# Hybrid layers and recurrence of a 4-layer network: slab splits ahead of the latents, angles in the second network, a new order behind the last recurrent tile

## What is computed

```python
def recurrent_mixer(x, ...):
    gate, xr = jnp.split(x @ w_in, [LRU_WIDTH], axis=-1)
    xr = causal_depthwise_conv(xr, conv_w, conv_b)
    r, i = sigmoid(block_diag(gate_a_w, gate_a_b)), sigmoid(block_diag(gate_x_w, gate_x_b))
    log_a = -LRU_C * r * softplus(-a_param)
    u = sqrt(-expm1(2.0 * log_a)) * (i * xr)
    h = scan(h -> exp(log_a) * h + u)
    return (h * gelu(gate)) @ w_out

def hybrid_layer(x, positions, ...):
    h = rms_norm_2(x, g_mix)
    (a_q, a_k, a_v, b_qlat, b_kvlat, b_krope, c_q, c_k, c_v, c_f, d_val, d_gate) = split(h @ w_in)
    out_a = chunk_band_attention(a_q, a_k, a_v, rel_bias)
    q  = rms_norm_2(b_qlat, g_q_lat) @ w_uq        # 64 + 32 columns a head; the 32 are rotated
    kv = rms_norm_2(b_kvlat, g_kv_lat) @ w_ukv     # keys (b_key) and values (b_values)
    k_rot = apply_rope(b_krope, positions)         # cos and sin of positions * inv_freq
    out_b = block_causal_attention(q, [kv keys, k_rot], kv values, CHUNK)
    out_c = block_causal_attention(c_q, c_k, c_v, 1, cumsum(log_sigmoid(c_f + b_forget)))
    out_d = silu(layer_norm(depthwise_conv(d_val * sigmoid(d_gate))))
    x = x + sum(sigmoid(h @ w_gate + b_gate) * (branches @ w_branch)) @ w_o
    return x + square(relu(rms_norm_2(x, g_ffn) @ w_up)) @ w_down
```

## Time and profile before

| | us |
|---|---|
| median of 3 runs | 2874.03 (2872.92 to 2875.7) |
| the profiled execution | 2871.91 |
| its span in the profile | 2870.1 |

### The profile page before, as it was taken

One profiled execution on the slowest core, in us unless ns is written; L12 is line 12 of the kernel. 1 busy time (PEld: TensorE's weight loads), 2 busy tenths in 40 slices (PEclk: granted clock), 3 DMA queues, 4 the chain that ended last, 5 costly groups with the idle time before them and its releaser, 6 DMA issues.

```text
span 2870.1 us, 32424 instructions
## 1 busy us (share of the span) xinstructions
PE 2799.6 (98%) x12948; PEld 2267.7 (79%) x12948; DVE 1248.2 (43%) x2084; ACT 1231.1 (43%) x1803; POOL 1234.4 (43%) x550
## 2 busy tenths in 40 slices
PE   8999999999989999998999999999989999999998
PEld 7786888888768888876777888888767777888886
DVE  4666551544675335335656432021256574330112
ACT  3665442434844334324673443133235754442331
POOL 4222444444554444433445444444424564444442
PEclk9999999999999999999999999999999999999999
DMA  4211232333223333322222323333322222333332
GB/s 149 89 63 63 89 103 94 96 103 96 81 81 96 103 95 96 103 81 74 74 67 88 96 96 96 98 98 98 96 73 81 61 88 88 96 96 101 97 96 73
DMA packets 73926, 259.21 MB, mean 90 GB/s; under 512 B 9184, under 2 KB 9184, under 8 KB 73776
## 3 DMA queue, kind: packets, MB, share of 16 engines
q1 hardware_dynamic: 71680, 251.79, 27.9%
q10 hardware_dynamic: 2096, 5.36, 0.5%
HBM read 254.95 MB, written 2.13 MB: 90 GB/s over the span
## 4 chain that ended last, share of the span: by engine, by line
PE 91%; DVE 4%; ACT 3%; POOL 1%; issue 1%; DMA 0%; SPq 0%; DVEq 0%; ACTq 0%; POOLq 0%
PE ps L423 27%; PE ps L425 26%; PE ps L424 26%; PE ps L489 2%; PE ps L519 1%; PE ps L502 1%; PE ps L544 1%; PE ps L546 1%; PE ps L545 1%; PE ps L434 1%; ACT w_hi L876 1%; PE ps L471 1%; PE ps L473 1%; PE ps L472 1%; POOL w_lo L1885 1%
## 5 line engine op out<-in xcount | busy, mean ns | idle before, releaser
L1885 POOL TENSOR_TENSOR w_lo<-raw,w_hi 128x1024 fp32r<-128x1024 f32 x470 | 1133.9, 2415 | 1516.8 <-ACT w_hi L876 1516.7
L423 PE MATMUL ps<-xs,w_hi 128*128 128x512 f32 x2176 | 864.7, 397 | 14.0 <-POOL w_lo L1885 11.2
L424 PE MATMUL ps<-xs,w_hi 128*128 128x512 f32 x2176 | 849.6, 390 | 0.0
L425 PE MATMUL ps<-xs,w_lo 128*128 128x512 f32 x2176 | 849.4, 390 | 0.0
L876 ACT ACTIVATE w_hi<-raw 128x1024 fp32r<-128x1024 f32 x470 | 493.8, 1052 | 620.7 <-PE ps L425 575.6
L423 PE MATMUL ps<-hid,w_hi 128*128 128x512 f32 x1320 | 517.8, 392 | 13.6 <-POOL hid L1909 9.7
L425 PE MATMUL ps<-hid,w_lo 128*128 128x512 f32 x1320 | 515.1, 390 | 0.0
L424 PE MATMUL ps<-hid,w_hi 128*128 128x512 f32 x1320 | 514.9, 390 | 0.0
L423 PEld LDWEIGHTS ps<-xs,w_hi 128*128 128x128 f32 x2176 | 410.2, 189 | 116.7 <-issue 12.8
L424 PEld LDWEIGHTS ps<-xs,w_hi 128*128 128x128 f32 x2176 | 410.2, 189 | 88.9 <-issue 5.0
L425 PEld LDWEIGHTS ps<-xs,w_lo 128*128 128x128 f32 x2176 | 410.0, 188 | 86.2
(11 more groups left out here) (213 smaller groups left out, 2610.8 us busy)
## 6 DMA issues: line engine op xcount, KB each, us to landing
raw<-in_weights SPq DMA_DIRECT2D x470, 512.0 KB, 3.5
hT<-in_x ACTq DMA_DIRECT2D x4, 512.0 KB, 9.5
btab<-in_rel SPq DMA_DIRECT2D x8, 256.0 KB, 3.6
out<-tmp ACTq DMA_DIRECT2D x8, 256.0 KB, 2.0
btab<-in_heads SPq DMA_DIRECT2D x6, 256.0 KB, 3.7
tmp<-in_heads SPq DMA_DIRECT2D x6, 256.0 KB, 4.2
common<-in_fixed ACTq DMA_DIRECT2D x1, 642.0 KB, 12.9
small<-in_small ACTq DMA_DIRECT2D x1, 368.5 KB, 4.7
```

What stands on the lines that cost most here:

```text
L423: pe.matmul(banks[bank][:], wh, rh, start=(k == 0), stop=False)
L424: pe.matmul(banks[bank][:], wh, rl, start=False, stop=False)
L425: last = pe.matmul(banks[bank][:], wl, rh, start=False, stop=(k == len(specs) - 1))
L1885: gp.tensor_tensor(w_lo[:, n % NPAIR, :], raw[:, n % NRAW, :], w_hi[:, n % NPAIR, :].bitcast(F32), ALU.subtract).then_inc(*w_low.tick(n))
```

## The change

In the hybrid layers ScalarE gets steps `("ahead", n)`: it opens the slab of c_head n between the latents' steps; the other engines skip them. b_values moves from attention step 1 to step 2, behind c_head 4. The by-token product uses bank 4 instead of 7, and b_key 0 uses bank 4 instead of the next of the ring.

The angles and their sine move into `network(1, 3)`, between the up tiles and the down tiles of its first half, and use `pbuf` instead of `tmp`.

In the recurrence Gelu of gate 7 moves on ScalarE behind the high part of tile 7's input; tiles 6 and 7 take Exp and Sqrt together; VectorE takes `rec_1(6)` before tile 7's low part; TensorE adds inputs 3, 4 and 5 one at a time over six outputs; ScalarE and GpSimd get one order written out for all of this. TensorE's products are the same in number. Unchanged lines are left out.

```diff
-                   ("latent_parts", 1), ("latent_parts", 0), ("c_head", 1), ("c_head", 2), ("c_head", 3)]
-        beside2 = {0: [("rope", 0)], 1: [("b_key", 0), ("b_key", 1), ("b_values", 0)], 2: [("c_head", 4)],
+                   ("ahead", 1), ("latent_parts", 1), ("ahead", 2), ("latent_parts", 0), ("ahead", 3), ("c_head", 1),
+                   ("c_head", 2), ("c_head", 3)]
+        beside2 = {0: [("rope", 0)], 1: [("b_key", 0), ("b_key", 1)], 2: [("c_head", 4), ("b_values", 0)],
...
-        rec_first = {8: [(0, 0, 3), (1, 0, 3)]}
-        rec_early = {8: [(o, 0, 3) for o in range(2, 6)], 9: [(o, 3, 5) for o in range(6)],
-                     10: [(o, 5, 6) for o in range(6)]}
@@ TensorE: root_by_token @@
-                wait_bank(7)
+                wait_bank(4)
...
-                free[7] = (vec, ("by_token", m))
+                free[4] = (vec, ("by_token", m))
@@ TensorE: recurrence @@
-            for c in range(13):
-                if c < 8:
-                    rec_0(c)
-                for o, k0, k1 in rec_first.get(c, ()):
-                    rec_out(o, k0, k1)
-                if 0 <= c - 1 < 8:
+            for c in range(8):
+                rec_0(c)
+                if c:
                     rec_1(c - 1)
-                for o, k0, k1 in rec_early.get(c, ()):
-                    rec_out(o, k0, k1)
+
+            for o in range(2):
+                rec_out(o, 0, 3)
+            rec_1(7)
+            for o in range(2, 6):
+                rec_out(o, 0, 3)
+            for k in range(3, 6):
+                for o in range(6):
+                    rec_out(o, k, k + 1)
@@ TensorE: hybrid, b_key @@
-                        bk = next_bank(("b_key", L, a))
+                        if a:
+                            bk = next_bank(("b_key", L, a))
+                        else:
+                            bk = bank_of["b_key", L, a] = 4
@@ ScalarE: network @@
+                    if L == 1 and part == 0:
+                        A.wait_ge(vec, "angles")
+                        ac.activation(rp[64:128, :], pbuf[64:128, 0, :], ACT.Sin).then_inc(*act.tick("rope"))
                     for o in range(8):
                         weights(("down", L, part, o))
@@ ScalarE: recurrence (rec_t is the third Tanh, taken out of rec_1) @@
+            roots_of = {3: (0, 1), 5: (2, 3), 7: (4, 5)}
+            for c in range(8):
+                weights(("rec_g", c))
...
+                weights(("rec_x", c))
+                if c < 7:
                     rec_gate(c)
...
+                rec_in(c)
+                if c:
                     rec_1(c - 1)
+                if 0 < c < 7:
+                    rec_t(c - 1)
+                rec_high(c)
+            rec_t(6)
+            rec_gate(7)
+            rec_4(3)
+            for o in range(2):
+                weights(("rec_out", o))
+            weights(("rec_a", 7))
+            weights(("rec_i", 7))
+            rec_1(7)
+            rec_t(7)
+            rec_2((6, 7))
+            for o in range(2, 6):
+                weights(("rec_out", o))
+            for k in range(3, 6):
+                rec_4(k + 1)
+                for o in range(6):
+                    weights(("rec_out", o), k)
+            rec_4(7)
@@ ScalarE: hybrid @@
-                    elif what == "c_head":
+                    elif what in ("c_head", "ahead"):
                         weights(("c_head", L, a))
@@ VectorE: network @@
+                    if L == 1 and part == 0:
+                        angles()
                     residuals((0, 1, 2, 3) * 2, ("down", L, part), m + 1 if part else None)
@@ VectorE: rec_0, and its loop @@
                     V.wait_ge(product, ("rec_i", c - 2))
+                if c == 7:
+                    rec_1(6)
                 take_low(hi_lo(hid, 8 + c % 2), xc, ("rec_x", c))
...
+            rec_3(4)
+            rec_1(7)
+            for c in range(5, 8):
+                rec_3(c)
@@ GpSimd: recurrence, behind tile 7 @@
+            rec_4(3)
+            for o in range(2):
+                weights(("rec_out", o))
+            weights(("rec_a", 7))
+            weights(("rec_i", 7))
+            rec_3(4)
+            for o in range(2, 6):
+                weights(("rec_out", o))
+            for k in range(3, 6):
+                rec_4(k + 1)
+                rec_3(k + 2)
+                for o in range(6):
+                    weights(("rec_out", o), k)
+            rec_4(7)
```

More of the change, by code:

```diff
@@ L448, in root_by_token @@
                 T.wait_ge(inverse, ("root", m))
-                wait_bank(7)
+                wait_bank(4)
                 for b in range(NB):
-                    t = pe.matmul(banks[7][:, b:b + 1], rt[0:1, P * b:P * b + P], ones[0:1, 3, 0:1], start=True, stop=True)
+                    t = pe.matmul(banks[4][:, b:b + 1], rt[0:1, P * b:P * b + P], ones[0:1, 3, 0:1], start=True, stop=True)
                 t.then_inc(*mean.tick(("by_token", m)))
-                free[7] = (vec, ("by_token", m))
+                free[4] = (vec, ("by_token", m))
             def values(group, specs, rhs, m, bank0):
@@ L1103, in rec_1 @@
             def rec_1(c):
-                e, t, gi = ring(c)
+                e = ring(c)[0]
                 A.wait_ge(product, ("rec_a", c))
@@ L1111, in rec_1, with rec_t @@
                     *act.tick(("rec_i", c)))
+            def rec_t(c):
+                e, t, gi = ring(c)
                 A.wait_ge(vec, "softplus")
@@ L1129, in rec_4 @@
                 take_high(hid[:, c, :], tmp[:, 4 + c % 4, :], ("rec_y", c))
-            roots_of = {3: (0, 1), 5: (2, 3), 7: (4, 5), 8: (6,), 9: (7,)}
-            for c in range(13):
-                if c < 8:
-                    weights(("rec_g", c))
+            roots_of = {3: (0, 1), 5: (2, 3), 7: (4, 5)}
+            for c in range(8):
+                weights(("rec_g", c))
                 if c == 0:
@@ L1161, in scalar @@
             network(1, 3)
-            A.wait_ge(vec, "angles")
-            ac.activation(rp[64:128, :], tmp[64:128, 4, :], ACT.Sin).then_inc(*act.tick("rope"))
             def hybrid(L):
@@ L1370, in by_token @@
                     V.wait_ge(moved, event)
-                ve.tensor_copy(rtok, banks[7][:, 0:NB]).then_inc(*vec.tick(("by_token", m)))
+                ve.tensor_copy(rtok, banks[4][:, 0:NB]).then_inc(*vec.tick(("by_token", m)))
             def values_out(group, event, bank0, dst):
@@ L1569, in softplus, with angles @@
                 ve.tensor_scalar(hb[:, 8:16], small[:, gx0:gx0 + 8], 0.5, None, ALU.mult).then_inc(*vec.tick("softplus"))
+            def angles():
+                r64 = slice(64, 128)
+                ang, kk = pbuf[r64, 0, :], pbuf[r64, 1, :]
+                V.wait_ge(l_pos, "pos")
+                V.wait_ge(l_common, "common")
+                chain(ve.tensor_copy(kk, rp[r64, :].bitcast(I32)))
+                V.wait_ge(step)
+                chain(ve.tensor_scalar(ang, kk, ropec[r64, 0:1], None, ALU.mult))
+                V.wait_ge(step)
+                chain(ve.tensor_scalar(kk, ang, 1.0 / (2 * math.pi), ropec[r64, 1:2], ALU.mult, ALU.add))
+                V.wait_ge(step)
+                chain(ve.tensor_scalar(kk, kk, 12582912.0, None, ALU.add))
+                V.wait_ge(step)
+                chain(ve.tensor_scalar(kk, kk, -12582912.0, None, ALU.add))
+                c1 = 6.28125
+                c2 = float(np.float32(2 * math.pi - c1))
+                c2 = float(np.frombuffer((np.frombuffer(np.float32(c2).tobytes(), np.uint32) & 0xFFFFF000).tobytes(), np.float32)[0])
+                c3 = 2 * math.pi - c1 - c2
+                for cc in (c1, c2, c3):
+                    V.wait_ge(step)
+                    chain(ve.scalar_tensor_tensor(out=ang, in0=kk, scalar=-cc, in1=ang, op0=ALU.mult, op1=ALU.add))
+                V.wait_ge(step)
+                chain(ve.tensor_scalar(ang, ang, ropec[r64, 2:3], 3.1415925, ALU.add, ALU.min))
+                V.wait_ge(step)
+                ve.tensor_scalar(ang, ang, -3.1415925, None, ALU.max).then_inc(*vec.tick("angles"))
             def network(L, m):
@@ L1640, in rec_3 @@
                 ve.tensor_tensor_scan(att[:, 8 + c, :], t, gi, 0.0, ALU.mult, ALU.add).then_inc(*vec.tick(("rec_scan", c)))
[L1642 removed]
+            for c in range(8):
                 if c == 0:
                     root(2)
[L1645 removed]
+                if c >= 4:
                     rec_3(c - 4)
[L1647 to L1650 removed]
+                scale(2 * (c % 2), ("rec_g", c), 2, ("rec_g", c))
+                rec_0(c)
+                if 0 < c < 7:
                     rec_1(c - 1)
+            rec_3(4)
+            rec_1(7)
+            for c in range(5, 8):
+                rec_3(c)
             residuals(range(8), ("rec_out",), 3, ("rec",))
             network(1, 3)
[L1656 to L1679 removed]
             def hybrid(L):
@@ L1912, in gpsimd @@
             through(("rec_g", 0))
-            for c in range(13):
-                if c < 8:
-                    weights(("rec_g", c))
```

(17 more changed lines are left out.)

45 lines of the change are left out of this document (2 added, 43 removed).

## The result

The changed kernel takes **2852.2 us** (median of four executions, 2851.8 to 2853.4) beside 2874.1 for the kernel before. The ratio is 0.9925, with a 95% interval of 0.9913 to 0.9938. That is 22.0 us faster, where 24.4 were forecast.

The account below looks back on a forecast made before the run. TensorE, busy 98% of the span, bounds the kernel, so only its waits and low-clock stretches yield time. Gains 20.3 + 2.1 - 2.0 + 4.0 = 24.4 us off the 2874.0 median give 2849.6 us, range 2841 to 2861.

Parts of the forecast that it names:

- 1 and 2, latents and banks: Hybrid layers: slab splits ahead of the latents gain 20.3 us (17 to 23), bank moves 2.1 (1 to 2.3).
- the loss today in the first hybrid layer: End of c_head 2 to first transpose: 21 us of work in a 36.2 us window, so 15.2 us lost.
- The charge of 1.5 us of lower clock for each new wait: Behind the new wait of about 2.15 us before score 2, each hybrid layer: 1.5 us lost (0 to 3.0).
- 3, angles: Second network: old place gives back 4.1 us, new place costs 4.1 of wait plus 2.0 clock; net -2.0 us.
- 4, recurrence: End of the recurrence: tile 7's low part 5.2 us earlier, less 1.2 for lower clock; gain 4 us (0 to 6).
- Part (a): Recurrence, before tile 7's input: VectorE's low part ends 1.8 us earlier, and the wait shrinks to about 1.2 us.
- The charge of 1.2 us for the clock: Recurrence: 1.2 us taken off the gain for lower clock behind a TensorE stand of 4.4 us.
- A: Rival: splits hide the wait, nothing new appears, score 2's wait and angles cost no clock; gain about 29, 2845; chance 0.17.
- B: Rival: wait before score 2 keeps clock low, 3 us more per layer, angles 1 more; gain 17, 2857; chance 0.15.
- C: Rival: VectorE and GpSimd's shared-port lock delays the recurrence, tile 7 at 813.5; gain there 1, 2853; chance 0.10.
- D: Rival: slower, a long stretch at 1.2 GHz follows the new stand at 978; 200 slow matmuls give 2892; chance 0.03.
- E: Rival: opening slabs ahead waits for a late release, delaying the latents' high parts; gain 6, 2868; chance 0.05.

Follow-up runs that it names:

- sin_later: Changed kernel with ScalarE's Sin of the angles moved behind its second call for down-tile slabs; 2847.1 us, 25.9 faster than the kernel before.
- hybrid_alone: Kernel before with only the hybrid-layer edits (slabs opened ahead of latents, b_values later, bank 4 uses); 2853.0 us, 20.0 faster than the kernel before.
- recurrence_alone: Kernel before with only the new order of the recurrence; 2868.3 us, 4.7 faster than the kernel before.
- tile4_first: Changed kernel with tile 4's high part ahead of two slab splits and its low part ahead of both w_lo; 2851.4 us, 22.0 faster than the kernel before.

## Why the prediction was right, step by step

The forecast of 2849.6 us lies 2.6 below the measured 2852.2, and 24.4 us were forecast for a gain of 22.0.

- **1 and 2, latents and banks: forecast 22.4, alone 20.0.** Every mechanism was as told: splits at 1284.75, 1289.68 and 1297.11, ahead of, between and behind the high parts, none of which they delay; no wait at c_head 3; none at the second layer's by-token product (from the start of the sum for the root to the start of this product 6.43 us, 8.61 before); a new wait before score 2 of 1.96 us for VectorE's minimum behind the rotation, forecast as 2.15; the minimum itself behind three rotation instructions, as counted. The step that was mis-sized is the loss today in the first hybrid layer, 15.2 us by the window. It held 3.0 us of lower clock which that one execution had and others of the same code had not. The charge of 1.5 us of lower clock for each new wait has the right size (up to 1.8 in the first layer and 0 in the second here, 1.8 and 3.6 in sin_later, none in hybrid_alone).
- **3, angles: forecast -2.0, alone -2.0.** The wait at the new place was forecast as 4.1 and is 4.22. Redoing the same count at the new place, with TensorE's release of the slab three before, gave it. The lower clock behind it lost 2.6 us, where 2.0 were charged; in the other profiled executions with this wait the mean of the 7.4 us behind it was 0.63 to 0.77, which is 2.7 to 1.7 us.
- **4, recurrence: forecast 4, alone 4.7, but not by the forecast's two terms.** The waits shrank by 3.0 us, not 5.2. Part (a) was right, since tile 7's input is waited for 1.06 us (forecast 1.2). Tile 4's low part came 0.7 us later than forecast (799.46 less the 2.1 of the late start, so 797.3, for 796.6) and from there to tile 7's it took 15.2 us instead of 13.8. The main cause of both is one: I let VectorE's instructions end only with GpSimd's, but left GpSimd's own at 2.4 and 1.3 us. They took 5.59 for the pair, and 3.32 for a single w_lo and 2.19 for a product behind it. The charge of 1.2 us for the clock is right against the trace it was made from: by counts 8 matmuls (1.8 us) more, which is the 3.0 of waits less 1.2. Against the other two executions of the old order it has the wrong sign: 60 us at 0.86 became 60 at 0.91, about 2 us won.
- **Rivals.** A (no clock costs) and B (latent gain half eaten) did not come: A needs no lower clock anywhere, B 4.5 us of it before score 2 in each layer, and there were 1.8 and 0, besides 2.6 at the angles. C, the lock, is true as a mechanism: the rows of 2.88 and 2.56 us stand beside the 5.59. Scan 7 ended at 804.3 in the times of before, a third of the way from the forecast's 802.5 to C's 808, and tile 7's low part at 812.5 is nearer to C's 813.5 than to my 810.4. The time it gave (gain 1) lies below the interval of recurrence_alone, 2.0 to 7.2, but it takes the clock to get there: waits less charge are 1.8. D and E did not happen: at most some 12 matmuls ran slow in one go behind the stand at 978, and the opening ahead never waited for a late release.
- **What would show it.** The signs given for parts 1 to 3 all came: no w_lo wait at c_head 3, 2 us before score 2, none near 1240, 4 us near 978, none at latent 0 and the transposes. Tile 7's low part was the one that missed.

That the total came out close owes something to luck. The first hybrid layer was over-counted by 3.0 us and the recurrence's gain in waits by 2.2, while its clock was under-counted by about 3 (2 won where 1.2 were charged): three misses that largely cancel.

## What to carry to other kernels

When an engine waits for a slow result and has cheap, already possible work for the busiest engine behind that wait, take this work ahead of the wait: two splits of 1 us each, taken ahead into gaps of about 4 us in each of two layers, were worth 17 us here (10 to 19 by execution), and taking Sin one call later removed its wait too. Which buffer releases the splits behind a slow wait have to follow says how late it may stand. Cost waits and clock apart. The waits of a given order were the same in every execution to 0.2 us in all (single ones of the recurrence differed by up to 0.4), and the low stretches behind them were not. And where two engines hinder each other, sorting the queue of one may gain nothing, as in tile4_first; taking work from the one that comes last gave 6.9 us.

## What the runs showed of the hardware

**The same wait, a different clock.** The wait before score 2 was 1.96 us in every profiled execution that had it. With nothing else waiting, the mean clock over the same 60 us was 0.97 or, in hybrid_alone, 1.00 in the first layer, and 1.00 or, in sin_later, 0.94 in the second. In the old order of the recurrence it was 0.94 or 0.86, in the new one 0.91 or 0.94. Each step of 0.03 is up to 1.8 us. A gain of 3 us read from one trace may be nothing else. The one kernel that was profiled twice, the changed one, had the same means both times (0.97, 1.00 and 0.91). What decides it in a given execution I have not found.

**GpSimd and VectorE hinder each other in both directions.** VectorE's tensor_scalar of 64 partitions took 0.49 us alone (at 973.34 above) and 2.52 beside a w_lo (in sin_later); its L1682 with two SBUF tiles 0.68 alone (at 802.09 in the changed kernel) and 2.88; its scan 1.22 and 3.24. The instruction with one operand in PSUM kept its 0.66 us (L1679 at 800.46, beside GpSimd's product). GpSimd's w_lo went from 2.4 to 3.32 us, its product from 1.30 (at 809.81, VectorE idle) to 2.19. The Trainium skill, "SBUF — State Buffer", section "Who interferes with whom", says that a VectorE instruction with two SBUF inputs contends with a GpSimd instruction that reads SBUF, that one with at most one SBUF input outside the two-port modes does not, and that the one that comes second stands for the whole of the other's instruction. The rows with two SBUF inputs agree, and so does the PSUM one. In tile4_first the scan at 798.97 ends at 802.2, 1.1 us behind the end of the w_lo begun before it, and GpSimd's low part at 801.08 ends 1.1 us behind the end of the scan: each took about its time alone (1.22 and 1.3 us), counted from the other's end. That is what the prediction left out of the rule: the second may as well be GpSimd. tensor_scalar has one SBUF input and was held up too; whether it ran in a two-port mode no row tells.
